# Differential attention: the projections of 16 heads as seven half-size products a pair of weight slabs, with the roots side by side and the tanh behind the next head's exponentials

## What is computed

```python
def project(u, n):
    q, k, v, z = jnp.split(u @ w_in, 4, axis=-1)
    q = rms_norm(q.reshape(bsz, n, 2 * DIFF_HEADS, DIFF_DH), qn_g)
    k = rms_norm(k.reshape(bsz, n, 2 * DIFF_HEADS, DIFF_DH), kn_g)
    ...
p = jax.nn.softmax(s, axis=-1)
w = p[:, :, 0] - lam * p[:, :, 1]
o = jnp.einsum('bhqk,bkhe->bqhe', w, v)
o = rms_norm(o, subln_g) * (1.0 - lam_init)
out = (o * jax.nn.silu(z)) @ w_out
```

## Time and profile before

| what | value |
|---|---|
| three runs | 3729.68, 3730.71, 3731.41 us, median 3730.71 |
| profiled execution | 3726.98 us, of which the span of the core 3725.1 us |
| busy over the span | PE 96%, DVE 50%, ACT 32%, POOL 8% |
| granted TensorE clock, mean | 0.988 |
| differential attention | from 1568.5 to 2674.3 us |
| its 14 equal steps | from 1694.13 to 2611.60 us |

### The profile page before, as it was taken

The page is one execution under the profiler, slowest core; times in us unless marked ns, Lnnn a source line. Parts: engine busy times, 40 slices in busy tenths (PEclk is TensorE's granted clock), DMA queues, the critical chain, the costliest instruction groups (busy, mean ns, idle before and its releaser), DMA issues.

```text
span 3725.1 us, 48285 instructions
## 1 busy us (share of the span) xinstructions
PE 3590.1 (96%) x17514; PEld 2490.5 (67%) x17514; DVE 1865.9 (50%) x3821; ACT 1182.8 (32%) x2199; POOL 306.3 (8%) x355
## 2 busy tenths in 40 slices
PE   8999999998999999899999999999897999999999
PEld 4455688874547888666666666666455888888874
DVE  5734553545646445434545445454304666666651
ACT  3113210112433001123444444444202555555540
POOL 6700000000000000000000000000001222222210
PEclk9999999999999999999999999999998999999999
DMA  8532334331123342411011111101011222222212
GB/s 175 153 81 61 103 101 113 91 104 27 33 68 102 97 118 80 120 35 34 29 34 34 30 32 34 34 28 34 29 51 48 63 62 57 57 61 62 62 48 62
DMA packets 456597, 246.46 MB, mean 66 GB/s; under 512 B 43264, under 2 KB 448512, under 8 KB 456480
## 3 DMA queue, kind: packets, MB, share of 16 engines
q1 hardware_dynamic: 441152, 215.79, 21.5%
q0 software_dynamic: 14144, 28.36, 2.8%
q10 hardware_dynamic: 1184, 0.71, 0.1%
HBM read 229.96 MB, written 14.80 MB: 66 GB/s over the span
## 4 chain that ended last, share of the span: by engine, by line
PE 90%; DVE 6%; ACT 2%; issue 1%; DMA 1%; SPq 0%; DVEq 0%; ACTq 0%
PE bank L559 20%; PE bank L1874 13%; PE bank L401 10%; PE bank L2426 10%; PE bank L1860 5%; PE bank L1317 3%; PE bank L1142 3%; PE bank L2445 3%; PE bank L1897 2%; PE bank L965 2%; PE bank L1191 2%; PE bank L1212 2%; PE bank L1842 2%; PE bank L942 1%; PE bank L1884 1%
## 5 line engine op out<-in xcount | busy, mean ns | idle before, releaser
L1874 PE MATMUL bank<-hT,ring 128*128 128x512 f32 x1504 | 510.1, 491 | 1.0 <-ACT arena L2077 1.0
L1874 PEld LDWEIGHTS bank<-hT,ring 128*128 128x128 f32 x1504 | 278.5, 190 | 218.5 <-issue 204.7
L401 PE MATMUL bank<-big,ring 128*128 128x512 f32 (+1 forms) x1024 | 394.0, 541 | 1.1 <-DVE big L2203 1.1
L401 PEld LDWEIGHTS bank<-big,ring 128*128 128x128 f32 x1024 | 191.5, 190 | 176.7 <-issue 168.8
L2476 POOL TENSOR_TENSOR tb<-ring 128x512 f32<-128x512 f32 x32 | 40.6, 1268 | 2812.0 <-DVE big L2952 2649.2
L1198 ACT ACTIVATE arena<-bank 128x512 f32<-128x512 f32 (+2 forms) x224 | 118.4, 528 | 408.4 <-PE bank L1191 407.5
L559 PE MATMUL bank<-big,arena 128*128 128x256 f32 x1024 | 228.8, 379 | 0.0
L559 PEld LDWEIGHTS bank<-big,arena 128*128 128x128 f32 x1024 | 194.6, 190 | 26.5
L2104 DVE TENSOR_REDUCE cols<-bank 128x1 f32<-128x768 f32 x128 | 116.5, 952 | 149.7 <-PE bank L1842 149.6
L1860 PEld LDWEIGHTS bank<-ring,hT 128*128 128x128 f32 x1536 | 175.2, 192 | 12.5 <-issue 12.5
L1860 PE MATMUL bank<-ring,hT 128*128 128x128 f32 x1536 | 178.3, 276 | 0.0
(11 more groups left out here) (343 smaller groups left out, 6103.9 us busy)
## 6 DMA issues: line engine op xcount, KB each, us to landing
ring<-in_mlp_w SPq DMA_DIRECT2D x128, 512.0 KB, 5.5
ring<-in_a_w_in SPq DMA_DIRECT2D x64, 512.0 KB, 4.0
ring<-in_b_w_in SPq DMA_DIRECT2D x64, 512.0 KB, 4.1
ring<-in_mod_w SPq DMA_DIRECT2D x48, 512.0 KB, 5.2
ring<-in_even_w_in SPq DMA_DIRECT2D x32, 512.0 KB, 5.0
bias_d<-tb POOLq DMA_DIRECT2D x96, 128.0 KB, 3.7
big<-bias_d POOLq DMA_DIRECT2D x16, 768.0 KB, 5.2
ring<-in_a_w_out SPq DMA_DIRECT2D x16, 512.0 KB, 4.0
```

What stands on the lines that cost most here:

```text
L401: mm = pe.matmul(bk(self.bank(n, j))[:, 0:z - a], ring[s][:, k % KT, :], self.rhs(k, a, z), start=k == order[0], stop=k == order[-1], skip ...
L1874: mm = pe.matmul(flatb[2][:, a:z], ring[s][:, k, :], hT[:, k, a:z], start=k == 0, stop=k == KT - 1)
```

## The change

A pair of slabs (q and k, then v and z) is taken as a 2 x 2 arrangement of blocks, the 512 tokens as two halves of 256 columns, and the product is made with seven products of half size instead of eight (Winograd's form of Strassen's scheme): P1, P5, P6, P4, P2, P3, P7, each four matmuls of 256 columns (`products`). Four of the seven weight operands are sums or differences of blocks (S1 to S4), now made by POOL for each pair (`pool_dif`); the sums of the token blocks (T1 to T4) are made once on DVE ahead of the phase (`dve_sums`), T1 in place in `hT`. The context's 256 columns stay out of the scheme and are multiplied in the usual way (`context`). ACT copies P1 and P5 aside (`copied`), and DVE puts the results together (`sum2`, `first_half`, `last_half`, `second_tile`).

v is now made like z, with its width on partitions, so six transposes (`values`, name "vt") and an ACT copy turn it. The slabs of the phase are `ring[0]` to `ring[3]` for every head instead of two sets in turn; `ring[4]` to `ring[7]` hold the sums. The four stretches of PE's row become P1 to P3 of q and k; P7, a rotation and the context of q and k; P1 to P3 of v and z with the other rotation and the sums of squares; P7 and the context of v and z. The root for q stands behind the square of k, right ahead of the root for k ("roots together"). z's tanh moves to the next step, behind `exps(0)`, and `gate` behind `maxima(1)`. In the opening the context products of head 0 come first. In the last step the products of the output projection that are done early (`ahead`) are spread as 2, 1, 1, 2 and 3 where they were 3, 3 and 3.

```diff
-                ("dif", range(8), 8), ("wout2", range(8), 2),
+                ("dif", range(4), 16), ("wout2", range(8), 2),
...
+        dt_ = {T2: whole(ring[4]), T3: whole(ring[5]), T4: whole(ring[6])}
+        dsum = {S1: whole(ring[7])[:, 0:S], S2: whole(ring[7])[:, S:2 * S]}
+        dsum[S4], dsum[S3] = dsum[S1], dsum[S2]
...
+        NPROD = {P1: ("A11", B11, "C"), P5: (S1, T1, "Y"), P6: (S2, T2, "X"), P4: ("A22", T4, "Z"),
+                 P2: ("A12", B21, "C"), P3: (S4, B22, "Y"), P7: (S3, T3, "X")}
...
+            def products(r, *xs):
...
+                    if x == P1:
+                        arrived(pe, "dif", 2 * r, g)
+                        arrived(pe, "dif", 2 * r + 1, g)
+                        pe.wait_ge(m_free, dth("free", 2, g, r))
+                        if r == 0 and h is not None:
...
+                    if x == P5 and r == 1:
+                        st.g_done(pe, "qk")
...
+                    if wt in dsum:
+                        pe.wait_ge(m_wsum, dth("wsum", 8, g, 4 * r + wt))
+                    if x == P6:
+                        pe.wait_ge(m_copied, dth("copied", 4, g, 2 * r + 1))
+                    if x == P4:
+                        pe.wait_ge(m_copied, dth("copied", 4, g, 2 * r + 2))
+                    if x == P2:
+                        pe.wait_ge(m_u2, dth("u2", 2, g, r + 1))
+                    if x == P7:
+                        pe.wait_ge(m_c11, dth("c11", 2, g, r + 1))
+                    for k in range(4):
+                        if wt in dsum:
...
+                            rhs = {B11: hT[:, k, 0:H], T1: hT[:, k, H:S], B21: hT[:, 4 + k, 0:H],
+                                   B22: hT[:, 4 + k, H:S]}[t]
...
+            def context(r, j):
...
+                elif j == 0:
+                    pe.wait_ge(m_u3, dth("u3", 2, g, r + 1))
+                for k in range(KT):
+                    mm = pe.matmul(ctx_bank(h, r)[:, C * j:C * j + C], ring[2 * r + j][:, k, :], hT[:, k, S:TT],
+                                   start=j == 0 and k == 0, stop=k == KT - 1, skip_group_check=True)
...
+            def values():
...
+                for t in range(6):
+                    mm = pe.transpose(flatb[3][:, P * t:P * t + P], v_raw[:, P * t:P * t + P], ident)
...
-            if not make:
+            if make:
+                products(0, P1, P5)
+            else:
...
+                ahead(0, 2)
+            if on:
+                values()
...
-                project(0, "q", 0, 4 if old else 8)
+                products(0, P6, P4)
...
-            if make and old:
-                project(0, "q", 4, 8)
...
-            ahead(3, 3)
             if make:
+                products(0, P7)
                 rotate_q()
-                project(1, "k", 0, 2)
+                if on:
+                    context(0, 0)
+            else:
...
-            if make:
-                project(1, "k", 2, 5)
-                stats_q()
-                project(1, "k", 5, 8)
+            if make and on:
+                context(0, 1)
...
             if make:
+                products(1, P1)
                 rotate_k()
-                project(2, "v", 0, 2)
+                products(1, P5)
+                stats_q()
+                products(1, P6, P4)
                 stats("sk", st.sq["k"], b64[:, 48:80])
-                project(2, "v", 2, 6)
+                products(1, P2, P3)
...
-                project(3, "z", 0, 2)
+                products(1, P7)
                 broadcast("bk", st.rr["k"])
-                project(3, "z", 2, 8)
+                if on:
+                    context(1, 0)
+                    context(1, 1)
...
+            def copied(r, x):
...
+                act.activation(dp1 if x == P1 else dp5, dtwo[r].C if x == P1 else dtwo[r].Y, ACT.Copy)\
+                    .then_inc(m_copied, 1)
...
+            def tanh():
+                act.wait_ge(ds["nr"], h + 1)
+                act.wait_ge(m_y, dth("y", 2, h, 1))
+                act.wait_ge(m_c2, dth("c2", 2, h, 2))
+                act.activation(d_raw, dz_(e), ACT.Tanh, scale=0.5).then_inc(m_y, 1)
...
                 exps(0)
+                tanh()
                 turned(0, h)
+            if make:
+                copied(0, P1)
+            if on:
+                exps(1)
+            if make:
+                copied(0, P5)
+            if on:
+                values()
...
+            def sum2(r):
...
+                dve.wait_ge(m_copied, dth("copied", 4, g, 2 * r + 1))
+                dve.wait_ge(m_c2, dth("c2", 2, g, r))
+                dve.tensor_tensor(du, dp1, w.X, ALU.add).then_inc(m_u2, 1)
...
+            def first_half(r):
...
+                dve.wait_ge(m_prod, dth("prod", 14, g, 7 * r + P2))
+                dve.tensor_copy(dst_[:, 0:H], w.C).then_inc(m_c11, 1)
...
+            def last_half(r):
...
+                dve.wait_ge(m_u2, dth("u2", 2, g, r + 1))
+                dve.tensor_tensor(dst_[:, H:S], du, w.Y, ALU.add).then_inc(m_c12, 1)
...
+            def second_tile(r):
+                w = dtwo[r]
+                dst_ = dz_(ge) if r else d_raw
+                dve.wait_ge(m_prod, dth("prod", 14, g, 7 * r + P7))
+                dve.wait_ge(m_c12, dth("c12", 2, g, r + 1))
+                dve.tensor_tensor(du, dp1, w.X, ALU.add).then_inc(m_u3, 1)
+                dve.wait_ge(m_u3, dth("u3", 2, g, r + 1))
+                dve.wait_ge(m_copied, dth("copied", 4, g, 2 * r + 2))
+                dve.tensor_tensor(dst_[:, 0:H], du, w.Z, ALU.subtract).then_inc(m_free, 1)
+                dve.tensor_tensor(dst_[:, H:S], du, dp5, ALU.add).then_inc(m_c2, 1)
...
+            def context_qk():
+                if h is None:
+                    dve.wait_ge(m_prod, dth("prod", 14, g, P1))
+                else:
+                    multiplied(dve, "dif", 1, g)
+                b = ctx_bank(h, 0)
+                dve.tensor_copy(d_q[:, S:TT], b[:, 0:C])
+                dve.tensor_copy(d_raw[:, S:TT], b[:, C:2 * C]).then_inc(ds["gf"], 1)
...
                 maxima(1)
+                gate()
                 probs(1)
+            if make:
+                sum2(0)
             if old:
...
+            if make:
+                first_half(0)
...
                 inverse("so'", "o'")
             if make:
-                evac(0, d_q)
+                last_half(0)
             if on:
...
-                rotated_q()
+                second_tile(0)
+                turned_q()
...
-                evac(1, d_raw)
+                context_qk()
+                rotated_q()
             if on:
                 maxima(3)
             if make:
                 rotated_k()
+                sum2(1)
...
                 inverse("sk", "k")
+                first_half(1)
+                last_half(1)
...
+            if make:
+                second_tile(1)
+                normed_k()
+            if on:
...
             def one(g, e, u):
                 for j in range(4):
-                    load(sp, "dif", 4 * e + j, u, wd[:, :, j, bass.ds(g * P, P)])
...
+        def pool_dif(pool):
...
+                        if x == S1:
+                            arrived(pool, "dif", 2 * r, g)
+                            arrived(pool, "dif", 2 * r + 1, g)
+                        else:
+                            pool.wait_ge(m_wsum, dth("wsum", 8, g, 4 * r + x - 1))
...
+                        i0, i1, op = {S1: (block(b, 0), block(b, 4), ALU.add),
+                                      S2: (dsum[S1], block(a, 0), ALU.subtract),
+                                      S4: (block(a, 4), dsum[S2], ALU.subtract),
+                                      S3: (block(a, 0), block(b, 0), ALU.subtract)}[x]
+                        pool.tensor_tensor(dsum[x], i0, i1, op).then_inc(m_wsum, 1)
...
+            def t4(x):
+                return dst[x].rearrange("p (k n) -> p k n", k=4)
+            sub(t4(T3), h(4, H), h(0, H), 1)
+            sub(h(0, H), h(0, H), h(0, 0), 2)
```

More of the change, by code:

```diff
@@ L1836, in scores @@
                     pe.wait_ge(ds["nr"], h + 1)
+                    if first:
+                        pe.wait_ge(ds["gf"], 1)
+                        pe.wait_ge(m_y, dth("y", 2, 0, 1))
                 pe.wait_ge(ds["ex"], h * 5 + (t + 1))
@@ new lines, in products @@
+            def products(r, *xs):
+                w = dtwo[r]
+                acc = {"C": w.C, "X": w.X, "Y": w.Y, "Z": w.Z}
+                opening = h is None and r == 0
+                for x in xs:
+                    wt, t, o = NPROD[x]
+                    if x == P1:
[3 more added lines that the diff above has]
+                        if r == 0 and h is not None:
+                            pe.wait_ge(ds["gf"], st.g0 + (1 if old else 0))
+                        if opening:
+                            pe.wait_ge(n_out, res3.pre.k + 4)
+                    if x == P5 and r == 1:
+                        st.g_done(pe, "qk")
+                    if opening and t in (T1, T2, T4, T3):
```

(42 more changed lines are left out.)

195 lines of the change are left out of this document (105 added, 90 removed).

## The result

| | before | after |
|---|---|---|
| median | 3730.19 us (3728.18 to 3731.41, 4 runs) | 3667.51 us (3664.14 to 3669.0, 4 runs) |
| ratio | | 0.9834, 95% interval 0.9823 to 0.9846 |
| span of the profiled execution | 3725.1 us | 3667.3 us |

What follows compares the result with a forecast made beforehand. PE was taken to bound the 14 equal steps; savings of 58.8 us there, 4.1 in the first step and 17.8 in the opening made 80.7 us, for a forecast of 3650 us, range 3642 to 3674.

Steps and rivals of the forecast that it cites:

- What bounds the kernel: In the 14 equal steps: a step of 65.53 us is a sum of PE work, with 0.3 us of PE waits.
- The walk of the new waits: PE's row against DVE's in a step: the softmax chain of 6.5 us a chunk stays hidden behind PE's work.
- all three close places: In a step, context(0, 0), context(1, 0) and P2 of q and k have slack of 0.3, 0.4 and 1.3 us.
- The tanh's term (0.3): Ahead of pv' in each step: with z's tanh moved, ACT is 0.9 us earlier and PE's 0.3 us wait goes.
- The step that failed: PE work per step: 42.8 us out; products 24.2, context products 13.8 and transposes 0.7 in; 4.1 us saved.
- The hand-overs (0.2): At the close places in each step: 0.2 us lost a step, bounds 0 and 1.5.
- The opening: Before the first scores: scores(0) at 1613.4 instead of 1631.2, 17.8 us earlier, bounds 13 and 19.
- the prediction's signs of being wrong: PE waits for DVE before P2 or context, DVE operations over 1.5 us beside 2473, low clock in 1569-1583, ring-load waits.
- The first step: The step after the opening: 4.1 us saved, as it has no pv' and no 0.3 us wait to win.
- what was costed at nothing: Across the phase: DVE's under 4 us more a step, POOL's 10.2 us of sums and one set of slabs cost nothing.
- the first rival: In the steps: POOL's sums hold up sum2(0), up to 1.3 us a step, 18 us, giving 3668 us; 18%.
- The second rival: In the steps: each of 18 new pieces costs a 0.2 us gap, 3.6 us a step, giving 3700 us; 6%.

Runs made afterwards that it cites:

- the first three experiments: On the changed kernel: GpSimd's weight sums start later, 3663.72 us; broadcast bo' moved behind scores(3), 3660.76 us; GpSimd's eight weight sums a step left out, 3663.34 us.

## Why the prediction came out as it did

- **What bounds the kernel**: right. PE's row is the step, before and after, and PE has no wait in 14 steps.
- **The walk of the new waits**: right at all three close places. No wait for sum2 or the second tile stands in PE's list. (P1 and its copy, 1.73 + 0.37, are 2.1 and not 2.2; it decides nothing.) The tanh's term (0.3) was confirmed by undoing it.
- **The step that failed: "These prices hold only if PE passes from product to product without a gap", with 1.73 and 3.46 from the earlier trace rows.** Those rows stand behind full-size matmuls. In the new order seven of the new pieces of a step stand behind a small tile form. Products 25.27 us instead of 24.22, context products 14.25 instead of 13.84: +1.46. Two rotations now behind full-size work at 0.86 instead of 1.05: -0.38. The hand-overs (0.2) did not come: -0.2. Sum 0.88 a step, and 62.21 - 61.33 = 0.88. In 14 steps this is 12.3 of the missing 19.0 us. The cost was in the trace of before, in the rotation's own 1.05 (it stands behind scores there), and unseen in a projection's total. The experiments show the price and its places, not what the array does in that time.
- **The opening**, 4.9 us short and with 12.9 just outside its bounds of 13 and 19: 3.7 by GpSimd's first sums beside the residual's DVE chain and PE's lower clock behind the wait that they made, a place at which the walk did not look (it asked about sums only beside probs). Two of the prediction's signs of being wrong show it: DVE operations of over 1.5 us beside line 2473 (in each step L2366 is one too, with 1.69, but it costs PE nothing), and a low clock just ahead of 1573. The rest is 45.3 us from the first context product to scores(0) instead of 44.2: the same changes of form, a wait of 0.2, and 1.78 instead of 1.5 at the end. Doing the context products first is worth 8.8 us by the experiment.
- **The first step**, 2.2 us short: 0.9 as in every step; the rest is the clock behind the 4.28 us pause, 0.50 and 0.74 granted in 1624 to 1632. The kernel before has the same pause and a low clock behind it too (scores(1) 2.57 us, T0 1.49), but in the changed kernel it lasted longer (2.93, 1.54, and 4.51 for the two products instead of 3.62). In the first three experiments and the one on the tanh, which leave this stretch as it is and in which the low clock reached hardly more than scores(1) and T0, it took 59.5 to 59.7 us from scores(0) to the next Tc', about 3.1 less than the kernel before, which is 4.1 - 0.9. How long the clock stays low there is not the change's doing as far as these runs show.
- **The last step** and **what was costed at nothing** (loads, GpSimd's time, one set of slabs): right. DVE's own work rose by 5.3 us a step (528.29 / 14 against 454.20 / 14) and not by under 4, without reaching PE.
- **The rivals.** The time, 3667.5, is almost that of the first rival (3668), and that is luck, since its mechanism had no part in the steps: without any sum a step takes the same 62.21 us. The range held the time by the same luck, as its upper part, 3660 to 3674, was there above all for that rival. The hold-up of DVE by GpSimd's sums itself is real here, and cost PE in the opening what it did not cost it in the steps. The second rival (0.2 us a piece) had the size right and the place wrong: seven of 18 pieces, those behind a change of tile form.

## What to carry to other kernels

When a big PE operation is cut into pieces and other work is put between them, price each piece by what stands ahead of it, from rows with the same neighbour, and put groups of the same tile form side by side. When work is given to an idle engine, look for what its first, unforced start falls beside, not only at the places where its result is wanted. A total that hits a rival's number does not show the rival's mechanism: take the suspected work out and look at the step.

## What the runs showed of the hardware

- A change between full-array fp32 matmuls and groups on 64 rows costs 0.19 to 0.20 us each way (a product behind scores 1.92 instead of 1.73, a broadcast 0.85 behind the full array and 0.65 behind scores), as long as one weight load (0.19). Behind sums of squares on all rows and 32 columns a full-array product is late by the same 0.19 (two take 3.65 instead of 3.46). The Trainium skill ("TensorE: Matmul & The Clock Gate", section "The mechanism" in its part on packing small matmuls) says that a weight load is pulled ahead of matmuls under way where its row group is not theirs, or into the background buffer. The trace shows both cases: a load behind full-array matmuls, whose rows it shares, began 0.37 us before they ended, which fits the background buffer, while the full-array load behind scores, whose rows it shares too, began only 0.07 us before they ended. Why no load went ahead there, no run here shows.
- A group of matmuls on four column tiles takes 0.46 us with four matmuls and 0.45 with two; the four matmuls of a broadcast, in two row halves, 0.65 behind scores, and on all rows 1.30.
- DVE operations of 0.74 and 0.68 us took 1.76 and 1.75 beside GpSimd's first two sums, and the two sums 4.12 us together instead of 2.67: both sides lose. The Trainium skill ("SBUF — State Buffer", section "Who interferes with whom") calls the shared port pair an exclusive lock; the trace agrees: the first sum (from 1561.59) began 0.03 us behind a DVE operation that kept its 0.74 us, and the DVE operation that began at 1562.83, with that sum under way, took 1.76.
- Behind a pause of 4.28 us PE's clock was granted at 0.50 (the 1.2 GHz level) for a stretch, in some executions for longer than in others: the same code took 1.54 or 0.98 us for T0 and 4.51 or 3.62 for two products in different executions. The last step, with its pauses, took 44.9 to 47.2 us from Tc' to Tc in kernels that do not differ in it.
